# Two tiles at a time: rounded weights of both first, then their remainders, in all products of 512 columns

## The reference

```
# block 1
h = rmsnorm(x)*(1+scale)+shift;  proj = h @ w_in          # 2048 x 6160
y = [gated causal convolution | gated linear attention] @ w_out
x = x + gate * rmsnorm(y)
u = causal_dwconv3(h2 @ w_up)                             # 2048 x 11264
x = x + gate * rmsnorm((silu(u1)*u2) @ w_down)            # 5632 x 2048
# block 2
proj = h @ w_in_2                                         # 2048 x 8192
y_a = multiscale_pool(u) @ w_a_up;  y_b = stick_breaking_attention(q,k,v) @ w_b_up
x = x + gate * ((sigmoid(g_a)*y_a + sigmoid(g_b)*y_b) @ w_o)
x = x + gate * (relu(h2 @ w_ff1)**2 @ w_ff2)              # 2048 x 8192, 8192 x 2048
```

## Time and profile before

| | us |
|---|---|
| median of 3 runs | 2501.51 (2500.34 to 2504.88) |
| profiled execution | 2499.89 |
| its span, first to last instruction | 2498.6 |
| TensorE products, busy | 2463.8 (99%), 15172 instructions |
| TensorE weight loads, busy | 2193.7 (88%), 15177 instructions |
| VectorE busy | 1978.0 (79%) |
| ScalarE busy | 1260.2 (50%) |
| DMA | 652.14 MB, mean 261 GB/s |

### The profile page before, as it was taken

The page is one execution under the profiler, slowest core; times in us unless marked ns, Lnnn a source line. Parts: engine busy times, 40 slices in busy tenths (PEclk is TensorE's granted clock), DMA queues, the critical chain, the costliest instruction groups (busy, mean ns, idle before and its releaser), DMA issues.

```text
span 2498.6 us, 38060 instructions
## 1 busy us (share of the span) xinstructions
PE 2463.8 (99%) x15172; PEld 2193.7 (88%) x15177; DVE 1978.0 (79%) x2618; ACT 1260.2 (50%) x1861; POOL 5.9 (0%) x13
## 2 busy tenths in 40 slices
PE   7899999999999999999999999999999999999999
PEld 4699999988888888889988888888988888888888
DVE  6879989979977888889978788988688756656555
ACT  4354445555555555545545566554454444444443
POOL 0000000000000000000000000000000000000000
PEclk9999999999999999999999999999999999999999
DMA  9998889677767778777558677887578655555554
GB/s 381 408 343 301 336 337 344 214 252 262 261 243 280 261 249 296 250 262 265 184 207 324 219 290 276 314 322 282 184 278 315 245 190 186 187 188 196 188 185 135
DMA packets 135250, 652.14 MB, mean 261 GB/s; under 512 B 13041, under 2 KB 49905, under 8 KB 70305
## 3 DMA queue, kind: packets, MB, share of 16 engines
q1 hardware_dynamic: 133970, 645.06, 71.6%
q0 software_dynamic: 672, 3.31, 0.4%
q10 hardware_dynamic: 432, 1.35, 0.2%
HBM read 647.58 MB, written 2.10 MB: 260 GB/s over the span
## 4 chain that ended last, share of the span: by engine, by line
PE 94%; DMA 4%; DVE 1%; issue 1%; ACT 1%; SPq 0%; DVEq 0%; ACTq 0%
PE PM L622 46%; PE PM L623 23%; PE PM L619 5%; PE PM L620 5%; PE PM L621 5%; DMA raw<-in_w_mod 3%; PE PS L652 2%; PE PS L648 2%; PE PS L649 2%; PE PM L667 1%; PE PS L704 1%; PE PS L705 1%; PE PS L706 1%; PE PS L789 0%; DMA X<-in_x 0%
## 5 line engine op out<-in xcount | busy, mean ns | idle before, releaser
L1343 DVE TENSOR_TENSOR WL<-raw,WH 128x1024 fp32r<-128x1024 f32 (+1 forms) x865 | 998.4, 1171 | 413.1 <-ACT WH L954 411.7
L954 ACT CAST WH<-raw 128x1024 fp32r<-128x1024 f32 (+1 forms) x865 | 865.8, 1010 | 908.3 <-PE PM L623 663.0
L622 PE MATMUL PM<-H,WH 128*128 128x512 f32 x2944 | 1027.1, 394 | 0.0
L623 PE MATMUL PM<-H,WL 128*128 128x256 f32 x2944 | 822.1, 279 | 0.0
L622 PEld LDWEIGHTS PM<-H,WH 128*128 128x128 f32 x2944 | 551.5, 187 | 125.6 <-issue 0.3
L623 PEld LDWEIGHTS PM<-H,WL 128*128 128x128 f32 x2944 | 555.2, 189 | 0.1
L1350 DVE CUSTOM_DVE_ANT_0 raw<-raw,cb 128x2048 f32<-128x2048 f32 x192 | 438.4, 2284 | 17.4 <-DMA raw<-in_w_mod 16.7
L622 PE MATMUL PM<-FC,WH 128*128 128x512 f32 x1024 | 358.6, 393 | 0.0
L623 PE MATMUL PM<-FC,WL 128*128 128x256 f32 x1024 | 285.7, 279 | 0.0
L622 PEld LDWEIGHTS PM<-FC,WH 128*128 128x128 f32 x1024 | 191.9, 187 | 45.8
L623 PEld LDWEIGHTS PM<-FC,WL 128*128 128x128 f32 x1024 | 191.9, 187 | 0.0
(11 more groups left out here) (336 smaller groups left out, 3107.3 us busy)
## 6 DMA issues: line engine op xcount, KB each, us to landing
raw<-in_w_ff SPq DMA_DIRECT2D x128, 1024.0 KB, 4.9
raw<-in_w_in SPq DMA_DIRECT2D x110, 1024.0 KB, 6.5
raw<-in_w_mod SPq DMA_DIRECT2D x96, 1024.0 KB, 7.0
raw<-in_w_ada SPq DMA_DIRECT2D x96, 1024.0 KB, 5.9
raw<-in_w_up SPq DMA_DIRECT2D x80, 1024.0 KB, 5.1
raw<-in_w_down SPq DMA_DIRECT2D x64, 704.0 KB, 5.3
raw<-in_w_out SPq DMA_DIRECT2D x16, 1024.0 KB, 7.0
raw<-in_w_o SPq DMA_DIRECT2D x16, 1024.0 KB, 6.1
```

The source lines that it names most:

```text
L622: PE.matmul(bank(n)[:, :], wh, rhs, start=(kk == 0), stop=False)
L623: return PE.matmul(bank(n)[:, T:2 * T], wl, rhs[:, 0:T], start=False, stop=ends)
L954: S.copy(part(WH), w).then_inc(s_hi, 1)
L1343: V.tensor_tensor(part(WL), w, part(WH).bitcast(F32), ALU.subtract).then_inc(s_lo, 1)
```

## The change

A unit of a job that isn't folded now goes through a new function, `run_pairs`. It takes the tiles of the unit two by two. For both it issues the product of 512 columns with `WH`, then for both the product of 256 columns with `WL`. A unit of five tiles (the second one of a job with 11 tiles) has one tile left at its end, which runs as before. The wait on `s_lo` is at the start of the unit, as before, and the last product raises `s_unit`. `operand`, with its waits in a job that opens a stage, is called for both tiles ahead of the first product with `WL`. `run_tile` keeps the folded form alone.

```diff
@@ tensor() @@
-                if n in FOLDED:
-                    PE.matmul(acc(n), wh, rhs[:, 0:T], start=(kk == 0), stop=False)
-                    PE.matmul(acc(n), wh, rhs[:, T:2 * T], start=False, stop=False)
-                    return PE.matmul(acc(n), wl, rhs[:, 0:T], start=False, stop=ends)
-                PE.matmul(bank(n)[:, :], wh, rhs, start=(kk == 0), stop=False)
-                return PE.matmul(bank(n)[:, T:2 * T], wl, rhs[:, 0:T], start=False, stop=ends)
+                PE.matmul(acc(n), wh, rhs[:, 0:T], start=(kk == 0), stop=False)
+                PE.matmul(acc(n), wh, rhs[:, T:2 * T], start=False, stop=False)
+                return PE.matmul(acc(n), wl, rhs[:, 0:T], start=False, stop=ends)
+
+            def run_pairs(u):
+
+                PE.wait_ge(s_lo, u + 1)
+                for t in range(0, len(UNITS[u]), 2):
+                    tiles, moving = UNITS[u][t:t + 2], []
+                    for q, (n, kk) in enumerate(tiles):
+                        moving.append(operand(JOBS[n], kk))
+                        PE.matmul(bank(n)[:, :], WH[:, u % NUNIT, (t + q) * 128:(t + q + 1) * 128], moving[q],
+                                  start=(kk == 0), stop=False)
+                    for q, (n, kk) in enumerate(tiles):
+                        mm = PE.matmul(bank(n)[:, T:2 * T], WL[:, u % NUNIT, (t + q) * 128:(t + q + 1) * 128],
+                                       moving[q][:, 0:T], start=False, stop=(kk == JOBS[n].nk - 1))
+                mm.then_inc(s_unit, 1)
 
             def run(ls, which):
+                u = UNITS_OF[ls[0]][which]
+                if UNITS[u][0][0] not in FOLDED:
+                    run_pairs(u)
+                    return
```

## The result

The changed kernel takes 2507.48 us (median of 8 runs, 2506.79 to 2509.9) against 2501.52 us (8 runs, 2500.08 to 2504.88): a ratio of 1.0026, with a 95% interval of 1.0017 to 1.0035. The interval lies above 1, so the kernel is slower, by some 6 us. I had forecast 5 us less. The number is that of the milder form of my third rival, all pairs at 350 ns a tile (2508), but by luck: the trace has hardly a pair at 350 ns. It has 348.3 ns a tile over H and 353.3 over FC and MG.

What follows compares the result with a forecast made beforehand. TensorE's products, busy 99% of the span, were taken as the bound. 2464 pairs losing 2.0 ns each gave 4.9 us less, with loads, bank order and waits at 0: median 2501.5 to 2496.5 us, range 2489.5 to 2508.

Steps and rivals of the forecast that it cites:

- the milder form of my third rival: 512-column jobs: all pairs settle at 350.0 ns a tile, 6.4 us more, 2508.
- TensorE sets the time, and the change is worth what it does to the distances: 512-column jobs: both makers of weights are ahead, so only the distance from one product to the next counts.
- The sum for the waits on weights and on activations: Weights: nothing starts at another time, 0; activations in the ten opening jobs: 0, with 7.6 us kept for the range.
- The excess is what stands above 226.7 + 120.0: Mixed 512- and 256-column tiles: 3.3 ns in the middle and 6.7 in the slow cadence, together 9.9 us to win.
- I charge the excess to the change of size, so a pair loses half of it: Pairs have two size changes, not four: 2.0 ns less each, 2464 pairs, 4.9 us less; chance 0.38.
- The two cadences of H: H tiles run at 347 or 353.4 ns; uneven slow distances say the excess comes with the alternation in some phase.
- a size has one price among its like: Products following equal ones: 226.7 ns for 512 columns, 120.0 for 256, which the trace was said to support.
- Rival 1: The excess stays with the tile, nothing changes: 2501.5; chance 0.28, shared with the engine choosing its own product order.
- Rival 3: Pairs fall into a slow cadence: 23 us more (2524), or 6.4 us more (2508) at 350.0 a tile; chance 0.17.
- The rule weighed against it: Distance is columns over 2.4 GHz plus some 2.5 ns, whatever the neighbours: 325 ns a tile, no gain from reordering.

Runs made afterwards that it cites:

- experiment 4: TensorE alone, no transformer block computed: six product orders at several operand starts and lead-in products; the old order at start 0 took 346.7 or 353.3 ns a tile.
- experiment 6: Changed kernel with four tiles at a time (four products with `WH`, then four with `WL`), old starts: 2514.26 us, 1.0054 to the kernel before.
- experiment 7: Changed kernel with pairs only in jobs reading H: 2502.68 us, 1.0007; only in jobs reading FC, FB, YAB and MG: 2507.14 us, 1.0026.
- experiment 5: Operand starts moved by padding, ratios to the kernel before: changed kernel at start 64, 0.9911; old order at start 64, 1.0042; old order at start 32, 0.9938.

## Why the prediction was wrong, point by point

- *TensorE sets the time, and the change is worth what it does to the distances:* right. The waits on weights stayed where they were, but for 1.6 us at L618, and the distances hold 7.4 of the 10 us between the two profiled spans. The sum for the waits on weights and on activations (0 each) was right too.
- *The excess is what stands above 226.7 + 120.0:* this step failed first. I took each price from a stage in which the size has only its like around it: 226.7 from the value stage, where `WH` and `WL` move, at start 0, and 120.0 from the folded tiles over H. In the changed kernel 512 behind 512 is 233.8 ns at the mean, 7.1 over my price, and 256 behind 256 is 115.7, under it. Two things are wrong with the prices. They don't hold among other neighbours: at start 0, with TensorE alone, 512 behind 512 is 226.7 in a run of 512 columns and 233 in a run of pairs, and 256 behind 256 is 120.0 among folded tiles and 115 in pairs. And they don't hold at other starts: 512 behind 512, among its like, is 226.7 at start 0 and 233.5 at start 96, where FC, FB, YAB and MG begin. 346.7 is no floor for a tile either: pairs took 345.0 ns at start 64.
- *I charge the excess to the change of size, so a pair loses half of it:* wrong. By experiment 4 a product has no price that could be carried from one run of sizes to another. Four tiles at a time have half the changes and cost more (experiment 6), and the same run of sizes is 345.0 or 353.3 ns a tile by the start of its operand. I took the half for want of a row with the four-product pattern; the range held the outcome, the step did not.
- *The two cadences of H speak for the excess being a matter of phase:* right, and shown by experiment 4, which puts the same tiles at 346.7 or 353.3 ns by the product ahead of them.
- *Rival 1 (the place of the operand sets it):* right in half. The operand's place counts, but together with the order, so that a new order changes it all the same. I had seen that all tiles at 350 lay outside H and didn't look at where those operands start, which the declarations show.
- *Rival 3 (the new order falls into a slower cadence):* this is what happened, over FC and MG above all. Its mild form, all pairs at 350.0 ns a tile, was 6.4 us more, and the measured 6 us agree with it by luck: FC and MG went past it, to 353.3, and H stayed under it, at 348.3. By the summed distances 4.8 us of the loss lie over FC, MG, FB and YAB and 2.6 over H, where 348.3 stands for a mix of mostly 346.7 and some 353.3; the kernel with pairs over H alone (1.0007) can't be told from the kernel before.
- *The rule weighed against it:* the Trainium skill (TensorE: Matmul & The Clock Gate, Back-to-back issue gap) has a formula of the columns alone, which it gives for an isolated product; for a stream of weight loads and products of 512 columns the same section has some 131 ns. No row here agrees with either: 512 columns behind 512 go from 226.7 to 234.3 ns with the start of the operand, and a tile of 512 and 256 from 345.0 to 360.0. That a size has one price among its like, which I wrote that the trace agrees with, it doesn't bear out over other starts.

What stays open is the mechanism inside TensorE. The runs show what the cadence depends on: the order of sizes, the relative start of the two operands, and the phase in which a run of products is entered. They don't show why. Nor is it shown why pairs at start 64 take 345.0 ns alone and 346.7 in the whole kernel. The two are not the same place: the distance to the weights is 64 bytes modulo 256 alone and 192 in the kernel, and TensorE alone never ran at 192. At 32 and 160 pairs differ by 5 ns, so this may be all of it. Two cadences at one place, as H had before and FC has in experiment 7, would do it too. Which of the two it is was not tried.

## What to carry to other kernels

Where TensorE is never starved, read a product's distance from its starts in each stage, and look at where its operands begin before an order of products is judged: here padding is worth more than the order. It took 0.6% off the old order (32 bytes), and it took the pairs from 0.26% over the kernel before to 0.9% under it (64 bytes), where it cost the old order 0.4%. A distance between two products can't be carried to another operand or another neighbour. A small kernel with TensorE alone, on the addresses of the real one, gave in one run three of the four whole-kernel ratios of experiments 5 and 6 within 0.11%, and the fourth inside a range of 0.35%. But the sums of experiment 5 held terms that were off by several us and in part made up for each other, so it said which way a start or an order goes better than by how much. Its buffers should lie at the same distance from the weights modulo 256 bytes, and not only 128.

## What the runs showed of the hardware that I had not expected

- The start of an operand, in steps of 16 bytes, changes the rate of fp32r products by up to 6%: folded tiles 340.0 to 360.0 ns, 512-column products 226.7 to 234.3 ns. In the runs with TensorE alone what counts is the distance from the weights' start modulo 256 bytes. The Trainium skill (SBUF — State Buffer, Operand start alignment) asks only that an operand start at a multiple of its element size, and calls this a matter of legality and not of speed; by these runs a start that it allows can cost 6%.
- A run of products keeps its cadence over hundreds of tiles (552 tiles of H at 347 ns in one stretch of the kernel before), and what ran ahead of it chooses the cadence: in experiment 4 one product of 144 columns ahead and not 128 made 353.3 of 346.7 ns. All of this was at the upper level of TensorE's clock, with a granted clock of 0.998 to 1.0 in every run.
